# 480 unused bytes a partition behind a small tile, in a kernel of two transformer blocks on one core

## The reference

```python
def first_block(x, ...):                      # norms are rmsnorm
    h = rmsnorm(x, norm_mix)
    q, k, v, r, lr_f, lr_b, u, g_a, g_b = split(h @ w_in)            # 1024 x 5664
    o = gla(q, k, v, decay(lr_f)) + gla_backwards(q, k, v, decay(lr_b))   # 4 heads
    y_a = (head_norm(o) * gla_norm * silu(r)) @ w_branch_gla
    y_b = grouped(multiscale_pool(u), w_pool_group) * pool_scale
    x = x + (sigmoid(g_a) * y_a + sigmoid(g_b) * y_b) @ w_out
    gate, up = split(rmsnorm(x, norm_ffn) @ w_ffn_in)
    x = x + (silu(gate) * up) @ w_ffn_out
    return rmsnorm(x, norm_final)

def second_block(x, ...):
    h_ml, h_mla = mlstm(a @ w_in_2), attention(latents of a @ w_in_2)     # a = rmsnorm(x)
    x = x + rmsnorm(concat(h_ml, h_mla) @ w_out_2)
    x = x + rmsnorm(square(relu(rmsnorm(x) @ w_up_2)) @ w_down_2)
```

## Time and profile before

| what | value |
|---|---|
| median of 3 runs | 2840.65 us (2839.79 to 2842.64) |
| the profiled execution | 2838.5 us |
| its span, first to last instruction | 2836.8 us |
| TensorE busy (matmuls) | 2729.4 us, 96% |
| VectorE, ScalarE, GpSimd busy | 1814.4, 1021.3, 1277.9 us |
| mean granted clock of TensorE | 0.986 of full |
| moved by DMA | 348.90 MB, 123 GB/s on average |

### The profile page before, as it was taken

One profiled execution on the slowest core, in us unless ns is written; L12 is line 12 of the kernel. 1 busy time (PEld: TensorE's weight loads), 2 busy tenths in 40 slices (PEclk: granted clock), 3 DMA queues, 4 the chain that ended last, 5 costly groups with the idle time before them and its releaser, 6 DMA issues.

```text
span 2836.8 us, 32978 instructions
## 1 busy us (share of the span) xinstructions
PE 2729.4 (96%) x12578; PEld 2155.0 (76%) x12578; DVE 1814.4 (64%) x2070; ACT 1021.3 (36%) x1397; POOL 1277.9 (45%) x780
## 2 busy tenths in 40 slices
PE   7999999999999999999998999889998999999998
PEld 5888788787777888887786887555587788878777
DVE  3111355655747766669879758776637766777887
ACT  4000323332214333334444014665535433344444
POOL 2433322223436988884333444102332888833321
PEclk9999999999999999999999999999899999999999
DMA  5223232324442333336631534103333345565543
GB/s 180 96 95 108 88 119 90 119 90 156 148 141 79 100 112 102 90 118 215 205 115 49 187 112 117 33 33 97 102 127 104 119 141 163 173 206 163 163 134 134
DMA packets 336967, 348.90 MB, mean 123 GB/s; under 512 B 18915, under 2 KB 256602, under 8 KB 336822
## 3 DMA queue, kind: packets, MB, share of 16 engines
q1 hardware_dynamic: 327254, 311.30, 35.6%
q10 hardware_dynamic: 9568, 35.66, 3.2%
HBM read 237.53 MB, written 108.34 MB: 122 GB/s over the span
## 4 chain that ended last, share of the span: by engine, by line
PE 51%; DVE 10%; issue 2%; ACT 2%; DMA 1%; POOL 1%; SPq 0%; DVEq 0%; ACTq 0%; POOLq 0%
PE ps L3282 34%; PE ps L533 9%; DVE op_lo L3359 2%; PE ps L2367 1%; PE ps L2740 1%; DVE sw_lo L3192 1%; PE ps L2390 1%; DVE small L2321 1%; PE ps L2377 1%; DVE x L2312 1%; PE ps L2858 1%; DVE acc L3603 1%; DVE acc L3610 0%; PE ps L2713 0%; DVE acc L1889 0%
## 5 line engine op out<-in xcount | busy, mean ns | idle before, releaser
L3282 PE MATMUL ps<-op_hi,sw_hi 128*128 128x512 f32 x1769 | 692.6, 392 | 15.5 <-DVE op_lo L3359 8.2
L3282 PE MATMUL ps<-op_hi,sw_lo 128*128 128x512 f32 x1769 | 689.1, 390 | 0.0
L3282 PE MATMUL ps<-op_lo,sw_hi 128*128 128x512 f32 x1769 | 688.9, 389 | 0.0
L499 POOL TENSOR_TENSOR w_hi_t<-w_raw,ones 128x1024 fp32r<-128x1024 f32 (+1 forms) x85 | 162.1, 1910 | 735.7 <-PE ps L533 354.7
L3282 PEld LDWEIGHTS ps<-op_hi,sw_hi 128*128 128x128 f32 x1769 | 332.4, 188 | 96.8 <-issue 16.8
L3282 PEld LDWEIGHTS ps<-op_hi,sw_lo 128*128 128x128 f32 x1769 | 332.4, 188 | 69.2
L3282 PEld LDWEIGHTS ps<-op_lo,sw_hi 128*128 128x128 f32 x1769 | 332.6, 188 | 68.7 <-issue 0.5
L656 DVE TENSOR_TENSOR stage<-ps,rstd 128x1024 f32<-128x1024 f32 x62 | 75.8, 1222 | 345.4 <-PE ps L533 326.9
L3182 ACT ACTIVATE sw_hi<-sw_sumNone 128x512 fp32r<-128x512 f32 (+1 forms) x252 | 157.1, 624 | 330.3 <-PE ps L3282 247.0
L533 PE MATMUL ps<-h1hi,w_hi_t 128*128 128x512 f32 x720 | 233.5, 405 | 13.0 <-DVE h1lo L617 9.0
L3192 POOL TENSOR_TENSOR sw_lo<-sw_sumNone,sw_hi 128x512 fp32r<-128x512 f32 x138 | 214.7, 1565 | 33.2 <-ACT sw_hi L3182 33.1
(11 more groups left out here) (444 smaller groups left out, 4877.2 us busy)
## 6 DMA issues: line engine op xcount, KB each, us to landing
op_raw<-hidden SPq DMA_DIRECT2D x42, 1024.0 KB, 8.6
w_raw<-in_w_in SPq DMA_DIRECT2D x60, 512.0 KB, 3.9
sw_raw<-in_w_ffn_in SPq DMA_DIRECT2D x44, 512.0 KB, 5.3
proj<-stage ACTq DMA_DIRECT2D x42, 512.0 KB, 2.6
hidden<-hidden_blocks SPq DMA_DIRECT2D x13, 1536.0 KB, 6.2
acc<-proj SPq DMA_DIRECT2D x36, 512.0 KB, 4.5
hidden<-hidden_blocks SPq DMA_DIRECT2D x14, 1280.0 KB, 5.0
sw_raw<-in_w_up SPq DMA_DIRECT2D x32, 512.0 KB, 8.3
```

The source lines that it names most:

```text
L499: ins = pool.tensor_tensor(whi[:, u.par, s], raw[:, u.par, s], ones[:, 0:1].to_broadcast([P, n]), ALU.mult)
L3282: mm = pe.matmul(out, w, x[:, k, :], start=(k == 0 and i == 0 and r < 4), stop=(k == n - 1 and i == 2), skip_group_check=r >= 4)
```

## The change

```diff
--- before.py
+++ after.py
@@ -344,6 +344,7 @@
         emcol = sb("emcol", [P, 32])
         bytok = sb("bytok", [P, 6 * C])
         gg = sb("gg", [P, KT])
+        sb("to_whole_lines", [P, 120])
 
         def col(name, k):
             return cols[:, VEC[name] + k:VEC[name] + k + 1]
```

## The result

The kernel after takes 2823.13 us, the median of 4 runs (2822.41 to 2826.28), against 2840.86 us for the kernel before in its 4 runs: a ratio of 0.9939, interval 0.9924 to 0.9953, or 17.7 us less. The forecast was 2820.5 us, 20.1 us less. The profiled execution took 2822.44 us, with a span of 2820.7 us against 2836.8, which is 16.1 us less.

A forecast was written before the change was run, and what follows sets the result against it. TensorE, busy for 96% of the span, was taken as the bound; 3050 matmuls at 6.6 ns less give 20.1 us, and all other terms were put at zero, so 2840.65 us becomes 2820.5 us, range 2812 to 2829.

The forecast's parts named there:

- TensorE is full, so the cost of a matmul is paid.: Whole kernel: TensorE is busy for 96% of 2836.8 us, so each matmul's cost is paid almost in full.
- the sum: Matmuls on moved tiles: 3050 of 3456 save 6.6 ns each on the critical path, 20.1 us gained.
- 6.6 ns on each matmul of `h1`, `m2`, `m1`.: Matmuls on moved tiles: starts go from 233.3 to 226.7 ns apart, like those on `g1`.
- What is left is where in a line the read begins.: Moved operands: their own start address sets the matmul's time, a start on a multiple of 64 being what counts.
- What is free.: Matmuls before waits for `h1lo`, `ks`, split weights and smaller ones: 48, 192, 96 and about 70 bring no gain.
- The clock.: Stretches at 1.2 GHz: none in the sum; the range allowed one fall going away or two more, 6.2 us.
- The other users.: VectorE and ScalarE on moved tiles, plain fp32 matmuls and DMAs: taken as zero, at most about 1 us each.
- Rival A: Moved tiles: the start in a line is not the cause, so no change, 2840.65 us; chance 0.05.
- Rival B: Heads and `m2`: matmuls shorten but chains beside them absorb gain, leaving 12.0 us, about 2829 us; chance 0.10.
- Rival C: Longer waits make the granted clock fall more often; nine more stretches at 3.1 us give 2848 us; chance 0.03.

The follow-up runs named there:

- e2_pad96: Kernel after with 96 bytes of padding instead of 480, so the moved tiles begin on a multiple of 256; 2836.26 us, ratio 0.9985.
- e9_w160_x160: Against the kernel after: weight tiles moved 32 bytes to 160, `h1`, `m2`, `m1` at 160, `g1` and `op` left at 128; 2856.54 us, ratio 1.0053.
- e12_after_timed: The kernel after, unchanged, run once more; 2822.06 us as a median of 4, ratio 0.9944.
- e8_g1lo_off32: The kernel after with `g1lo` alone moved by 32 bytes, `g1hi` left in place; 2828.22 us in one execution.

## Why the prediction was right, and where it was not

- **TensorE is full, so the cost of a matmul is paid.** Right. Between 52 and 319 us the lead grew by 7.5 us, against 7.6 in the sum, and TensorE's busy time fell by 21.0 us with the same 12578 instructions.
- **6.6 ns on each matmul of `h1`, `m2`, `m1`.** Right on `h1` and `m1` (233.3 to 226.7), 6.0 on `m2` (to 227.3). 912 matmuls on `m2` at 0.6 ns less are 0.5 us of the miss.
- **"What is left is where in a line the read begins."** This is the step that failed. The prediction took the two facts of the trace, 160 slow and 128 fast, for a rule on the operand's own address, and supported it by 33 pieces of 64 bytes against 32. `e2_pad96` (a multiple of 256, 232.5 ns) and `e9_w160_x160` (160 fast, 128 slow) contradict it. In its place the runs show the distance to the weights modulo 256: 226.7 ns at 0, 228.9 at 64, 232.5 at 128, 233.3 at 32 and 96, and 233.3 at 224. The sum did not rest on the reading: it took its 6.6 ns from `g1`, whose operand and weights lie as those of the moved tiles do after the change. The reading as a rule gave the right time only because the weights happen to lie at 128, which was luck. The prediction ruled the weights out with "which are `w_hi_t` and `w_lo_t` for all"; that the same tiles take part in all cases does not remove them, if the cause is a relation between two addresses.
- **What is free.** Nearly right. The longer waits for `ks` and for the weights were predicted, as was the unchanged wait for `stage`. By the table above, with the stretches at 1.2 GHz left aside, the heads gave some 4.5 us instead of 5.1 (in `e12_after_timed`, which has the same 6.83 us at 1.2 GHz there as before), `m2` and `m1` of block 1 3.7 (in the same trace, which has no fall there) instead of 4.2, and block 2's `m2` 2.4 instead of 3.3. Together some 2 us of the 20.1 did not come.
- **The clock.** The prediction allowed for one fall that goes away and for two more, and put none in the sum. All three happened in the profiled execution, +2.3, -1.4 and -1.3 us, and nearly cancelled; that they did was luck. (The +2.3 is the 2.5 of the table less the 0.2 that `e12_after_timed` gains there with no such help.) With the wait on `op_lo` (-1.1) and the later start (-0.6) this gives 20.1 - 2 - 0.4 - 1.1 - 0.6 = 16.0, against 16.1 seen; the medians differ by 17.7.
- **The other users.** Right: the groups of VectorE, ScalarE and GpSimd kept their times (1813.5, 1020.3 and 1280.0 us busy).
- **Rival A, no change.** It fell. The rule beside it, the Trainium skill, page "SBUF — State Buffer", section "Door 1: The DMA port swizzle", with lines of 16 bytes, does not tell these cases apart: all distances tried but 16 and 48 are multiples of 32, and they give four different values. **Rival B** fell in its size: the heads kept 4.5 of 5.1 us. **Rival C** was seen in small: two new stretches, one of them right behind the wait it named, at 1.4 us each, not nine at 3.1.

What stays open is the mechanism. PEld is busy beside PE, so that each matmul's operand is read while the next weights are, and `e8_g1lo_off32` shows that a neighbour's distance counts; a conflict of two reads over the same part of the memory would fit that. It would also have to give the uneven steps of that run. No run here separates the two reads in time, so this is argued and not shown. It was not tried whether distances of 160 and 192 are like 96 and 64, as 224 is like 32, nor what a distance of 256 does, nor why `m1` at 128 is slower than `h1` and `m2`.

## What to carry to other kernels

Where TensorE is full and each matmul of 512 float32r columns has its own weight load, place the moved operands a multiple of 512 bytes from the weight tiles (256 may do, and was not tried); here it was worth 6.6 of 233.3 ns, 2.8% of each such matmul, for a pad of 480 bytes. Compare the distance of starts by operand tile within one kernel: two families with the same helper and shape and different spacing are a free experiment. And before calling an address the cause, move the other operand of the pair as well.

## What the runs showed that was not expected

- The cost depends on two addresses and not on one, and not evenly: 0, 2.2, 5.8 and 6.6 ns at distances of 0, 64, 128, and 32, 96 or 224.
- At 1.2 GHz the distance costs nothing. Two matmuls on `m1` of the kernel after, at distance 0, in the stretch at 793.87 us:

```profile
795.53 1.05 PE L534 MATMUL ps<-m1hi,w_lo_t 128*128 128x512 f32 x2
796.38 1.04 PE L534 MATMUL ps<-m1hi,w_hi_t 128*128 128x512 f32 x2
```

  That is 0.85 us for two, 425 ns each, the same as at distance 32 in the earlier trace rows; over all such stretches the steps on `h1` and `m1` average 426.6 ns before and 426.7 after. The plain fp32 matmuls on `kT` show none either. Their moving tile goes from distance 32 to 0 by the change (the weights are slices of `acc`, at 128), and their median stays 591 ns as in the earlier trace rows:

```profile
L2368 PE MATMUL ps<-kT,acc x192: 272/591/1223, 1764.6 to 1927.6; 96*128 96x512 f32 x96, 96*128 96x128 f32 x32, 96*128 96x256 f32 x32, 96*128 96x384 f32 x32
```
- A third of the operand reads at distance 32 brings two thirds of the cost, 4.4 of 6.6 ns.
- The stretches at 1.2 GHz move between executions of one kernel, 74.4, 88.1 and 83.8 us in total in three traces of the kernel after. At 427 instead of 227 ns a matmul, the 13.7 us between the least and the most are worth up to 6.4 us where TensorE is full (an estimate); the spans of the three differ by 2.0.
